# RWKV pairs: one of the two forms of a block inverse is updated, in half its columns, and the other is had by transposes

## The chip, the cores and the metric

One program runs on one core of a Trainium2 chip. The time is device microseconds (us) of that core, from the first to the last work of an execution; a kernel's time is the median of its runs. The engines work in parallel, each through its own list of instructions in order, and wait for one another by semaphores: PE (TensorE) multiplies matrices out of SBUF into PSUM, DVE (VectorE), ACT (ScalarE) and POOL (GpSimd) work on SBUF tiles (DVE and ACT also read PSUM), SP and POOL issue DMAs.

## What is computed

The program is two blocks, one after the other, on 256 tokens of 2048 channels. The first is two layers of linear attention, delta rule and differential attention, and the change leaves it alone. The second mixes with an RWKV scan, a convolution and a Fourier transform and ends with a feed-forward part. The change is in the RWKV scan: 16 heads of 64, over 256 context and then 256 own tokens, forward and backward.

```python
def wkv_scan(r, w, k, v, kk, a, s0, reverse):
    def step(s, inp):
        r_t, w_t, k_t, v_t, kk_t, a_t = inp
        sa = jnp.einsum('bhij,bhj->bhi', s, -kk_t)
        s = (s * w_t[:, :, None, :] + sa[..., None] * (kk_t * a_t)[:, :, None, :]
             + v_t[..., None] * k_t[:, :, None, :])
        return s, jnp.einsum('bhij,bhj->bhi', s, r_t)
    ...
def rwkv_mix(streams, s0, ln_w, ln_b, r_k, g_up):
    ...
    yf, sf = wkv_scan(r, wf, kf, v, kk, af, s0[0], False)
    yb, sb = wkv_scan(r, wb, kb, v, kk, ab, s0[1], True)
    y = yf + yb
    ...
def second_block(...):
    ...
    yc_rw, s_ctx = rwkv_mix(..., (s_zero, s_zero), *out_args)
    yx_rw, _ = rwkv_mix(..., s_ctx, *out_args)
```

## The kernel before

The scan is done in chunks of 64 tokens. Within a chunk the steps depend on one another through a unit triangular 64x64 matrix, and its inverse turns the recurrence into a few matrix products; from chunk to chunk only a 64x64 state is handed on. Two heads make a pair, one head on each half of the 128 partitions, and the 8 pairs are worked off one after the other. A pair has 8 cells (chunk and head) on each partition half and two directions d, so 32 systems of 64x64.

Of a direction's systems the tiles are: aT (the system), xm (its inverse), xmT (the inverse turned, that is transposed), mT (the part of aT that a level uses, by a mask), pm (a product copied out of PSUM), bT, rpk, kbv and wu (for what follows). Each is 128 partitions x 512 columns. PS is PSUM, eight banks of 512 columns.

The inverse is built by doubling. It starts with blocks of 2x2, and each of five levels joins two neighbouring blocks: with M the part that couples them, X becomes X - X M X. In the code a level has these steps, for d = 0 and d = 1 each:

- P: PE multiplies M and X (L1952, 64x64 products on quadrants of the array), into PSUM.
- ACT copies P to pm (`products`, L2255).
- X and Y: PE multiplies P from either side (L1969 for xm, L1971 for xmT), 64x64 columns each.
- DVE subtracts the two results from xm (L2631) and xmT (L2632), 512 columns each; level 5 needs xmT alone.
- POOL makes the next level's mT (`masks`, L1533) as soon as P has been read.

Ahead of level 1, PE makes scores of the pair (L1907 and L1909 for the system in both forms, L1919 and L1923 for the others) and, with the system copied, its turned form once more in another place (`turned_starts`, L1935); DVE masks them into the start values (`starts`). Level 5 also holds bT times the values (L1950), which ACT copies to kbv.

Around the levels, PE, DVE and ACT hold work of other pairs, written out by hand between the levels: head means and variances of the pair before (L1978 and the lines behind it) around levels 1 and 2, key sums of the next pair (L1866) after level 2, the decays of its two directions (L1858, L1859) after level 3 and inside or after level 4, key norms (L1873) after level 5. For each direction of decays ACT reads PE's result twice (a sigmoid and a multiple), DVE makes a running sum (`sums`, L2574 a scan, L2576 a product), and later ACT takes three exponentials; this goes into the scores of the next pair, which PE does after this pair's `solved` (L1991), eight dependent `steps` (L2001 to L2033), state updates (L2043) and outputs (L2053). The transposes by token (L1895) lie between the state updates.

Each engine works strictly in the order written; nothing reorders at run time apart from PE's weight loads. Semaphores named p_... count: p_P, p_Pc, p_Y, p_sub, p_xm, p_mask for the steps of a level, p_sig for the sigmoids, p_bvc for kbv. A matrix product in 32-bit floats is recorded as two MATMULs and two weight loads (LDWEIGHTS), a transpose as one of each.

## Time and profile before

| what | us |
|---|---|
| median of 3 runs | 3133.24 |
| lowest and highest run | 3127.13, 3143.53 |
| the profiled execution's own time | 3129.88 |
| its span in the trace | 3128.1 |

All rows are of that one profiled execution. Times in a timeline are microseconds from the start of the span, so that row times can be subtracted from one another. The RWKV pairs lie between about 1,635 and 2,165 us; the seven windows shown below each go from the scores of one pair to those of the next. The idle time before an instruction and what ended it stand in square brackets; "issue" there means that the engine waited for nothing that the profile shows. L numbers are lines of the kernel before.

### The profile page before, as it was taken

What the parts mean: (1) busy time and instruction counts of PE and PEld (TensorE: products, weight loads), DVE (VectorE), ACT (ScalarE), POOL (GpSimd) and SP (SyncE); (2) the same over time, 40 slices, a digit from 0 to 9 for tenths busy, and PEclk for the clock granted to TensorE, in tenths of its full rate; (3) what the DMA queues carried; (4) which work ended last, traced back from release to release, by engine and by line L of the source; (5) the groups of instructions that cost most, each with busy time, mean ns of one, the idle gap of its engine ahead of it and who ended that gap; (6) DMA issues with size and microseconds to landing.
All of it is one profiled execution on the core that took longest, in us unless ns stands there. A gap on an engine that the chain in (4) does not pass through costs nothing.

```text
span 3128.1 us, 68978 instructions
## 1 busy us (share of the span) xinstructions
PE 2990.7 (96%) x31912; PEld 2699.5 (86%) x31912; DVE 1603.6 (51%) x2262; ACT 566.0 (18%) x1041; POOL 1177.1 (38%) x657
## 2 busy tenths in 40 slices
PE   6999999999999999999998888888999999999998
PEld 5888888888888888787997777777999999999998
DVE  5755664656575324688914766765754131113232
ACT  1122111031110201100004555552110000000000
POOL 0000000100000000242772344443769787777775
PEclk9999999999999999999999999999999999999999
DMA  9954775955366445578640000002656444444442
GB/s 387 426 224 153 273 286 240 373 223 222 125 237 234 159 162 211 192 294 303 254 176 11 9 7 7 9 4 93 260 216 232 176 173 162 165 176 158 175 169 101
DMA packets 54160, 583.06 MB, mean 186 GB/s; under 512 B 6224, under 2 KB 6256, under 8 KB 8048
## 3 DMA queue, kind: packets, MB, share of 16 engines
q1 hardware_dynamic: 37856, 466.11, 39.3%
q0 software_dynamic: 16016, 112.54, 9.2%
q8 instruction: 251, 4.11, 0.5%
q14 instruction: 37, 0.30, 0.0%
HBM read 576.52 MB, written 2.10 MB: 185 GB/s over the span
## 4 chain that ended last, share of the span: by engine, by line
PE 90%; DVE 3%; issue 3%; DMA 2%; ACT 1%; POOL 0%; POOLq 0%; SPq 0%; DVEq 0%
PE PS L1766 28%; PE PS L371 20%; PE PS L1718 10%; PE PS L673 7%; PE PS L368 3%; PE PS L416 2%; PE PS L1952 2%; PE PS L1971 1%; PE PS L1969 1%; DMA ring<-in_w_start_dram 1%; PE PS L1895 1%; PE PS L1991 1%; PE PS L1783 1%; PE PS L1690 1%; PE PS L1701 1%
## 5 line engine op out<-in xcount | busy, mean ns | idle before, releaser
L371 PE MATMUL PS<-H,ring 128*128 128x256 f32 x2944 | 657.4, 381 | 0.0
L371 PEld LDWEIGHTS PS<-H,ring 128*128 128x128 f32 x2944 | 552.2, 190 | 82.7 <-issue 9.1
L1766 PE MATMUL PS<-H,ring 128*128 128x128 f32 x3424 | 402.8, 275 | 0.0
L1766 PEld LDWEIGHTS PS<-H,ring 128*128 128x128 f32 x3424 | 392.5, 192 | 0.1
L329 POOL DMA_DIRECT2D ring<-in_w_vec_dram x64 | 33.8, 528 | 860.2 <-DVE ring L930 659.1
L2463 DVE TENSOR_TENSOR W<-W,PS 128x256 f32<-128x256 f32 x58 | 24.4, 421 | 613.3 <-ACT W L2106 613.2
L1766 PE MATMUL PS<-H,W 128*128 128x128 f32 x2624 | 313.1, 275 | 0.0
L1766 PEld LDWEIGHTS PS<-H,W 128*128 128x128 f32 x2624 | 302.9, 192 | 0.0
L1585 POOL TENSOR_TENSOR W<-ring 128x1024 f32<-128x1024 f32 (+1 forms) x74 | 177.3, 2397 | 229.0 <-PE PS L1766 158.3
L673 PE MATMUL PS<-H,ring 128*128 128x256 f32 x1024 | 221.7, 379 | 2.9 <-DVE H L1228 2.9
L673 PEld LDWEIGHTS PS<-H,ring 128*128 128x128 f32 x1024 | 194.4, 190 | 30.0 <-issue 3.7
L1587 POOL TENSOR_TENSOR ring<-ring 128x1024 f32<-128x1024 f32 (+1 forms) x74 | 186.7, 2522 | 5.8
L1588 POOL TENSOR_TENSOR W<-W,ring 128x1024 f32<-128x1024 f32 (+1 forms) x74 | 180.7, 2442 | 0.0
L1590 POOL TENSOR_TENSOR W<-ring,W 128x1024 f32<-128x1024 f32 (+1 forms) x74 | 172.7, 2334 | 5.8
L1533 POOL TENSOR_TENSOR ring<-ring,W 128x512 f32<-128x512 f32 x64 | 89.0, 1408 | 185.0 <-PE PS L1952 185.0
L2199 ACT ACTIVATE ring<-PS 128x512 f32<-128x512 f32 (+2 forms) x248 | 130.6, 570 | 153.3 <-PE PS L1952 56.6
L2106 ACT ACTIVATE W<-PS 128x128 f32<-128x128 f32 (+2 forms) x60 | 17.0, 284 | 757.2 <-PE PS L1766 746.6
L930 DVE SCALAR_TENSOR_TENSOR ring<-ring,H 128x2048 f32<-128x2048 f32 x64 | 145.7, 2287 | 7.3 <-DMA ring<-in_w_vec_dram 6.6
L1718 PE MATMUL PS<-H,ring 128*128 128x128 f32 (+1 forms) x992 | 139.6, 302 | 5.5 <-DMA ring<-in_w_second_dram 5.4
L1718 PEld LDWEIGHTS PS<-H,ring 128*128 128x128 f32 x992 | 131.5, 195 | 12.2 <-DMA ring<-in_w_second_dram 5.5
L1766 PE MATMUL PS<-Pj,ring 128*128 128x128 f32 x1184 | 139.7, 275 | 0.0
L1766 PEld LDWEIGHTS PS<-Pj,ring 128*128 128x128 f32 x1184 | 135.9, 192 | 0.0
(472 smaller groups left out, 4915.6 us busy)
## 6 DMA issues: line engine op xcount, KB each, us to landing
ring<-in_w_second_dram SPq DMA_DIRECT2D x89, 2048.0 KB, 7.9
ring<-in_w_first_dram SPq DMA_DIRECT2D x68, 2048.0 KB, 7.9
ring<-in_w_vec_dram POOLq DMA_DIRECT2D x64, 1024.0 KB, 7.6
ring<-in_w_vec_dram SPq DMA_DIRECT2D x48, 1024.0 KB, 5.0
ring<-in_w_start_dram SPq DMA_DIRECT2D x16, 2048.0 KB, 15.8
Pj<-in_w_aside_dram SPq DMA_DIRECT2D x8, 2048.0 KB, 11.1
H<-in_w_vec_dram POOLq DMA_DIRECT2D x16, 1024.0 KB, 8.3
spare<-in_w_vec_dram POOLq DMA_DIRECT2D x16, 1024.0 KB, 8.6
```

What stands on the lines that cost most here:

```text
L368: mm = pe.matmul(PS[:, t % 2, half * TW:(half + 1) * TW], hT[:, k, half * P:(half + 1) * P], ring[:, t % 2, k, :], start=(k == 0), stop=(k ...
L371: mm = pe.matmul(PS[:, t % 2, half * T:(half + 1) * T], ring[:, t % 2, k, half * P:(half + 1) * P], hT[:, k, :], start=(k == 0), stop=(k = ...
L673: mm = pe.matmul(PS[:, 4 + 2 * (n % 2) + half, 0:T], ring[:, t % 2, k, half * P:(half + 1) * P], hT[:, k, :], start=(k == 0), stop=(k == K ...
L930: return v.scalar_tensor_tensor(out, a, s, b, op0, op1, **kw)
L1533: S("p_mask").inc(pool.tensor_tensor(mT[d], aT[d], each8(Ci(f"c_join{lev}")), ALU.mult))
L1585: sums.inc(pool.tensor_tensor(s_[:, 0], quarter(q, 2, nk), quarter(q, 3, nk), ALU.add))
L1587: sums.inc(pool.tensor_tensor(quarter(q, 2, nk), quarter(q, 0, nk), quarter(q, 2, nk), ALU.subtract))
L1588: sums.inc(pool.tensor_tensor(s_[:, 1], s_[:, 0], quarter(q, 0, nk), ALU.subtract))
L1590: sums.inc(pool.tensor_tensor(s_[:, 2], quarter(q, 1, nk), s_[:, 1], ALU.subtract))
L1718: mm = pe.matmul(in_regions(n % 2, wide, r), w[:, k * P:(k + 1) * P], at(m, k), start=(k == 0 and r // per not in opened), stop=(k == 7), ...
L1766: mm = pe.matmul(regions(bank2, r), w[:, k * P:(k + 1) * P], m[:, k, :], start=(first and k == 0 and r // 4 not in opened), stop=(last and ...
L2199: S(name).inc(act.activation(out_, in_, fn, **kw))
```

## The change

A level updates xmT alone. Its blocks of 2^lev columns come in two kinds, and the second of each two is all that a level alters; `joined` picks these, 256 of the 512 columns. Y multiplies 32 columns in place of 64 and X is gone. The product P is laid out so that all four quadrants of the array take part (`turned_at`, `by_parity`). xm is had by turning xmT: four transposes of 128x128 for each direction (`turned` in the program of PE), copied out of PSUM by DVE for d = 0 and by ACT for d = 1. There are five such turns for a pair, the first on the start values in place of `turned_starts`, and none after level 5.

With it go: only one start value for each direction on DVE; the first mT made by POOL, as a tenth mask; POOL's mask on rpk later, with a signal p_rpk of its own; the product of bT and the values in halves beside Y in levels 4 and 5, and its copies to kbv after p_sub of these levels; in ACT's `below` the copies of system and scores ahead of those to kbv. A direction's P now waits for one copy (p_xm or p_xs). Counting records of one pair, there are 280 MATMULs and 280 LDWEIGHTS fewer, out of 1,780 each.

The diff, without the tables of semaphores and their counts:

```diff
...
@@ -1406,6 +1406,9 @@
     GS = [flat(t)[:, 0:576].rearrange("p (m v) -> p m v", v=CH) for t in (Pj[:, 54:57, :], G[:, 5:8, :])]
     count = lambda lev, d: 2 * (lev - 1) + d + 1
     taken = lambda r, n: 2 * r + n + 1
+    turned_at = lambda u, c: 2 * (u // 2) + c
+    by_parity = lambda d: PS[:, 2 * d:2 * d + 2, 0:T]
+    joined = lambda t, lev: flat(t).rearrange("p (a s b) -> p a s b", s=2, b=1 << lev)[:, :, 1, :]
     seq = lambda t, d: t if d == 0 else t[:, :, ::-1]
 
 
@@ -1529,14 +1532,20 @@
 
         def masks(j, lev):
             for d in range(2):
-                need("p_P", j, count(lev - 1, d))
+                if lev == 1:
+                    need("p_aTc", j, d + 1)
+                else:
+                    need("p_P", j, count(lev - 1, d))
                 S("p_mask").inc(pool.tensor_tensor(mT[d], aT[d], each8(Ci(f"c_join{lev}")), ALU.mult))
 
-        def below(j, d):
+        def below_keys(j, d):
 
             need("p_BRr", j, d + 1)
             pool.tensor_tensor(bT[d], bT[d], each8(Ci("c_supper")), ALU.mult)
-            pool.tensor_tensor(rpk[d], rpk[d], each8(Ci("c_upper")), ALU.mult)
+
+        def below_reads(j, d):
+
+            return pool.tensor_tensor(rpk[d], rpk[d], each8(Ci("c_upper")), ALU.mult)
 
         def stream_back(j):
 
@@ -1559,12 +1568,15 @@
         ups(P, lambda ins: S("pair_loaded").inc(ins, 16))
         pool.wait_ge(S("cells_loaded").sem, 16)
         for j in range(NP2):
+            masks(j, 1)
             masks(j, 2)
-            below(j, 0)
+            below_keys(j, 0)
             masks(j, 3)
-            below(j, 1)
+            below_keys(j, 1)
             masks(j, 4)
+            below_reads(j, 0)
             masks(j, 5)
+            S("p_rpk").inc(below_reads(j, 1))
             if j < NP2 - 2:
                 need("p_z", j + 1, 2)
                 ups((j + 2) * P, lambda ins: ins.then_inc(S("pair_loaded").sem, 16))
...
@@ -1923,53 +1938,47 @@
                             mm = pe.matmul(PS[o_, 4 + 2 * d + par, T + n * CH:T + n * CH + CH], (pt, kt)[n // 2][r, t], RT(j, d)[r, tx], start=True, stop=True)
                 done(mm, "p_BR")
 
-        def turned_starts(j):
-
-            need("p_aTc", j, 2)
+        def turned(j, lev):
+
             for d in range(2):
-                kap, pt = flat(EV[d]), flat(AA[d])
-                for n in range(4):
-                    for c, o_ in enumerate(halves):
-                        t = slice(n * P + c * CH, n * P + c * CH + CH)
-                        for par, r in enumerate(halves):
-                            mm = pe.matmul(PS[o_, 2 + par, cell(4 * d + n)], pt[r, t], kap[r, t], start=True, stop=True)
-            done(mm, "p_xt")
+                if lev == 0:
+                    need("p_aTc", j, d + 1)
+                    need("p_x0", j, d + 1)
+                else:
+                    need("p_sub", j, count(lev, d))
+                for k in range(4):
+                    mm = pe.transpose(PS[:, 2 * d + k // 2, k % 2 * P:k % 2 * P + P], flat(xmT[d])[:, k * P:(k + 1) * P], ident)
+                done(mm, "p_xt")
 
         def level(j, lev, between=None):
-            if lev == 1:
-                turned_starts(j)
             for d in range(2):
-                if lev == 1:
-                    need("p_xs", j, d + 1)
-                else:
-                    need("p_mask", j, count(lev - 1, d))
-                    need("p_xm", j, count(lev - 1, d))
+                need(("p_xm", "p_xs")[d], j, lev)
+                need("p_mask", j, count(lev, d))
                 for u in range(8):
-                    if lev == 5:
-                        for h in halves:
-                            bv = pe.matmul(PS[h, 2 + d, cell(u)], bT[d][h, u, :], VTok[d][h, u % 4, halves[u // 4]], start=True, stop=True)
-                    for h, g in zip(halves, other):
-                        mm = pe.matmul(PS[h, d, cell(u)], mT[d][g, u, :], xm[d][g, u, :], start=True, stop=True)
-                if lev == 5:
-                    done(bv, "p_bv")
+                    g = halves[u % 2]
+                    for c, h in enumerate(halves):
+                        at = turned_at(u, c)
+                        mm = pe.matmul(PS[h, 2 * d + u % 2, cell(u // 2)], mT[d][g, at, :], xm[d][g, at, :], start=True, stop=True)
                 done(mm, "p_P")
             if lev == 1:
                 need("p_BRr", j, 1)
             for d in range(2):
                 need("p_Pc", j, count(lev, d))
-                if lev > 1:
-                    need("p_sub", j, count(lev - 1, d))
-                if lev == 1:
-                    need("p_x0", j, d + 1)
+                if lev == 5:
+                    need("p_bvc", j, d + 1)
                 if d and between:
                     between()
                 for u in range(8):
-                    if lev < 5:
-                        for h, g in zip(halves, other):
-                            pe.matmul(PS[g, 2 + d, cell(u)], xmT[d][h, u, :], pm[d][h, u, :], start=True, stop=True)
+                    if lev >= 4 and u < 4:
+                        w = 4 * (lev - 4) + u
+                        for h in halves:
+                            pe.matmul(PS[h, 4 + d, cell(4 + u)], bT[d][h, w, :], VTok[d][h, u, halves[lev - 4]], start=True, stop=True)
                     for h in halves:
-                        mm = pe.matmul(PS[h, 4 + d, cell(u)], pm[d][h, u, :], xmT[d][h, u, :], start=True, stop=True)
+                        out = PS[h, 4 + d, u * 32:(u + 1) * 32].rearrange("p (a b) -> p a b", b=1 << lev)
+                        mm = pe.matmul(out, pm[d][h, u, :], joined(xmT[d][h, u:u + 1, :], lev), start=True, stop=True)
                 done(mm, "p_Y")
+            if lev < 5:
+                turned(j, lev)
 
         def head_means(j):
             need("p_yread", j, 2)
@@ -1985,7 +1994,7 @@
         def solved(j):
             for d in range(2):
                 need("p_sub", j, count(5, d))
-                need("p_bvc", j, d + 1)
+                need("p_bvc", j, d + 3)
                 for u in range(8):
                     for h in halves:
                         mm = pe.matmul(PS[h, 4 * d + u // 4, (u % 4) * P:(u % 4 + 1) * P], xmT[d][h, u, :], kbv[d][h, u, :], start=True, stop=True)
@@ -2011,6 +2020,7 @@
                             mm = pe.matmul(PS[hs, sb_ + c, cell(n)], wu[d][rr, 4 * par + n, 0:64], PTok[d][rr, n, hs], start=True, stop=True)
                 done(mm, "p_rhs")
                 if d:
+                    need("p_rpk", j, 1)
                     need("p_rt", j, 1)
                 elif j < NP2 - 1:
                     need("p_kk", j + 1, 1)
@@ -2068,6 +2078,7 @@
         for r in range(4):
             by_token(0, r)
         scores(0)
+        turned(0, 0)
         for j in range(NP2):
             after, before = j < NP2 - 1, j > 0
             level(j, 1)
@@ -2094,6 +2105,7 @@
             outputs(j)
             if after:
                 scores(j + 1)
+                turned(j + 1, 0)
         head_means(NP2 - 1)
         head_vars(NP2 - 1)
 
@@ -2241,24 +2253,34 @@
                 need("p_tokT", j, taken(r, n))
                 f("p_tokc", t[d], PS[:, 2 + n, :].rearrange("p (a b) -> p a b", b=P), ACT.Copy)
 
+        def turned(j, lev):
+
+            need("p_xt", j, count(lev + 1, 1))
+            f("p_xs", flat(xm[1]).rearrange("p (b c) -> p b c", b=2), by_parity(1), ACT.Copy)
+
         def below(j):
 
+            for d in range(2):
+                need("p_aT", j, d + 1)
+                f("p_aTc", aT[d].rearrange("p (r n) b -> p r (n b)", r=2), PS[:, 2 * d:2 * d + 2, 0:T], ACT.Copy)
+            for d in range(2):
+                need("p_BR", j, d + 1)
+                f("p_BRr", br[d], PS[:, 4 + 2 * d:6 + 2 * d, :].rearrange("p r (w c) -> p r w c", w=2), ACT.Copy)
             need("p_tokc", j, 8)
             for d in range(2):
                 f("p_act", kbv[d].rearrange("p (r n) c -> p n r c", r=2)[:, :, :, 0:64], Ktok_[d].rearrange("p n (r c) -> p n r c", r=2), ACT.Copy)
-            for d in range(2):
-                need("p_aT", j, d + 1)
-                f("p_aTc", aT[d].rearrange("p (r n) b -> p r (n b)", r=2), PS[:, 2 * d:2 * d + 2, 0:T], ACT.Copy)
-                need("p_BR", j, d + 1)
-                f("p_BRr", br[d], PS[:, 4 + 2 * d:6 + 2 * d, :].rearrange("p r (w c) -> p r w c", w=2), ACT.Copy)
+            turned(j, 0)
 
         def products(j, lev):
             for d in range(2):
                 need("p_P", j, count(lev, d))
-                f("p_Pc", pm[d], PS[:, d, :].rearrange("p (a b) -> p a b", b=CH), ACT.Copy)
-                if lev == 5:
-                    need("p_bv", j, d + 1)
-                    f("p_bvc", kbv[d][:, :, 64:P], PS[:, 2 + d, :].rearrange("p (u c) -> p u c", c=64), ACT.Copy)
+                f("p_Pc", pm[d].rearrange("p (k b) c -> p b k c", b=2), by_parity(d).rearrange("p b (k c) -> p b k c", c=CH), ACT.Copy)
+            if lev < 5:
+                turned(j, lev)
+            if lev >= 4:
+                for d in range(2):
+                    need("p_sub", j, count(lev, d))
+                    f("p_bvc", kbv[d][:, 4 * (lev - 4):4 * (lev - 3), 64:P], PS[:, 4 + d, T:2 * T].rearrange("p (u c) -> p u c", c=64), ACT.Copy)
 
         def squares(j):
             need("p_yc", j, 1)
@@ -2608,30 +2630,30 @@
                 o.settle()
             o.do(v.tensor_tensor(EN[d], TMP[d], EN[d], ALU.mult), last)
 
+        def turned(o, j, lev):
+            need("p_xt", j, count(lev + 1, 0))
+            o.do(v.tensor_copy(flat(xm[0]).rearrange("p (b c) -> p b c", b=2), by_parity(0)), S("p_xm"))
+
         def starts(j):
             o = Order(v, own, j)
             for d in range(2):
                 need("p_AX", j, d + 1)
-                o.do(v.tensor_tensor(per_head(mT[d]), heads(2 * d, 0), each(Ci("c_join1")), ALU.mult))
-                o.do(v.tensor_tensor(per_head(xm[d]), heads(2 * d, T), each(Ci("c_join0t")), ALU.mult), S("p_aT"))
-                o.settle()
-                o.do(stt(xm[d], xm[d], -1.0, all8(Ci("c_ident")), ALU.mult, ALU.add), S("p_xs"))
-            need("p_xt", j, 1)
-            for e in range(2):
-                o.do(v.tensor_tensor(per_head(xmT[e]), heads(2, e * T), each(Ci("c_join0")), ALU.mult))
+                o.do(v.tensor_tensor(per_head(xmT[d]), heads(2 * d, T), each(Ci("c_join0")), ALU.mult), S("p_aT"))
             o.settle()
-            for e in range(2):
-                o.do(stt(xmT[e], xmT[e], -1.0, all8(Ci("c_ident")), ALU.mult, ALU.add), S("p_x0"))
+            for d in range(2):
+                o.do(stt(xmT[d], xmT[d], -1.0, all8(Ci("c_ident")), ALU.mult, ALU.add), S("p_x0"))
+            turned(o, j, 0)
 
         def level(j, lev, between=None):
             o = Order(v, own, j)
             for d in range(2):
                 need("p_Y", j, count(lev, d))
-                if lev < 5:
-                    o.do(v.tensor_tensor(xm[d], xm[d], bankv(2 + d), ALU.subtract), S("p_xm"))
-                o.do(v.tensor_tensor(xmT[d], xmT[d], bankv(4 + d), ALU.subtract), S("p_sub"))
+                o.do(v.tensor_tensor(joined(xmT[d], lev), joined(xmT[d], lev),
+                                     PS[:, 4 + d, 0:T].rearrange("p (a b) -> p a b", b=1 << lev), ALU.subtract), S("p_sub"))
                 if d == 0 and between:
                     between()
+            if lev < 5:
+                turned(o, j, lev)
 
         def centred(j):
             o = Order(v, own, j)
```

On PE, this is the place between levels 3 and 4 of a pair, with the decays of the next pair's first direction (L1858, L1859) between them; before, X (L1969) and Y (L1971) alternate in twos, 16 times in a level, of which the ends stand here:

```order
L1971 MATMUL PS<-ring 64x64 x2
L1969 MATMUL PS<-ring 64x64 x2
L1971 MATMUL PS<-ring 64x64 x2
L1858 MATMUL PS<-Pj,W 128x512
L1859 MATMUL PS<-Pj,W 128x512
L1952 MATMUL PS<-ring 64x64 x32
L1969 MATMUL PS<-ring 64x64 x2
L1971 MATMUL PS<-ring 64x64 x2
```

After, on the same engine and place, from Y of level 2 over the key sums (L1878) and the first direction's decays (L1870, L1871) to P of level 4:

```order
L1978 MATMUL PS<-ring 64x32 x32
L1950 MATMUL PS<-con,ring 128x128 x8
L1878 MATMUL PS<-con,W 128x2 x4
L1961 MATMUL PS<-ring 64x64 x32
L1978 MATMUL PS<-ring 64x32 x32
L1950 MATMUL PS<-con,ring 128x128 x8
L1870 MATMUL PS<-Pj,W 128x512
L1871 MATMUL PS<-Pj,W 128x512
L1961 MATMUL PS<-ring 64x64 x32
```

The turns (L1950) close a level, so that whatever was written behind a level now stands behind its transposes too, the decays of both directions included; before, they stood behind X and Y.

On ACT, the end of a pair before, from the copies of P in level 4 to the copies of `solved` (128x4x64 x8); the rows on W and H serve the next pair, 128x8x64 are the copies to kbv:

```order
L2199 ACTIVATE ring<-PS 128x512 x2
L2199 ACTIVATE W<-W,small,rope 128x512
L2199 ACTIVATE H<-H 128x512
L2199 ACTIVATE W<-PS,rope 128x512 x2
L2199 ACTIVATE ring<-PS 128x512
L2199 ACTIVATE ring<-PS 128x8x64
L2199 ACTIVATE ring<-PS 128x512
L2199 ACTIVATE H<-PS 128x8x64
L2199 ACTIVATE W<-W,small,rope 128x512
L2199 ACT_TABLE_LOAD
L2199 ACTIVATE W<-W 128x512 x3
L2199 ACTIVATE ring<-PS 128x4x64 x8
```

After, on ACT, the same place from the turn of level 4 on (128x512 out of PS), where 128x4x64 to ring and to H are the copies to kbv of levels 4 and 5:

```order
L2211 ACTIVATE ring<-PS 128x512
L2211 ACTIVATE ring<-PS 128x4x64
L2211 ACTIVATE H<-PS 128x4x64
L2211 ACTIVATE W<-W,small,rope 128x512
L2211 ACTIVATE H<-H 128x512
L2211 ACTIVATE W<-PS,rope 128x512 x2
L2211 ACTIVATE ring<-PS 128x2x4x64 x2
L2211 ACTIVATE ring<-PS 128x4x64
L2211 ACTIVATE H<-PS 128x4x64
L2211 ACTIVATE W<-W,small,rope 128x512
L2211 ACT_TABLE_LOAD
L2211 ACTIVATE W<-W 128x512 x3
```

The copies to kbv of level 5 stood between the two copies of P, ahead of Y; they now stand behind both and wait for DVE's subtraction of level 5, and the product on W, the table load and the exponentials stand behind them.

## Rows read from the trace of the kernel before

**Rows 1.** The page: totals, busy time of each engine, instruction queue, chain by engine.

```profile
span 3128.1 us, 68978 instructions
...
PE 2990.7 (96%) x31912; PEld 2699.5 (86%) x31912; DVE 1603.6 (51%) x2262; ACT 566.0 (18%) x1041; POOL 1177.1 (38%) x657
...
q8 instruction: 251, 4.11, 0.5%
...
PE 90%; DVE 3%; issue 3%; DMA 2%; ACT 1%; POOL 0%; POOLq 0%; SPq 0%; DVEq 0%
```

**Rows 2.** Windows of pairs: busy us by engine (instructions), granted clock, DMA share, GB/s.

```profile
1872.50:1932.30 59.80, 50.17 (x1782) 43.98 (x1779) 40.96 (x76) 32.02 (x56) 25.28 (x22) 1.00 0.03 7
1932.30:1993.20 60.90, 51.59 (x1784) 44.86 (x1781) 41.67 (x76) 31.93 (x56) 25.89 (x22) 0.97 0.03 7
...
sum 416.70, PE 352.50 PEld 307.64 DVE 283.62 ACT 225.06 POOL 178.25; mean PE 50.36 PEld 43.95 DVE 40.52 ACT 32.15 POOL 25.46
```

**Rows 3.** PE's waits from 1700 to 2160: total, times, longest.

```profile
PE PS L1971 <- issue: 17.1, 19, 1.8
...
PE PS L1969 <- issue: 6.5, 6, 1.6
...
PE PS L1907 <- issue: 0.6, 1, 0.6
```

**Rows 4.** PE's timeline of one pair: start, duration, line, shape, records.

```profile
1878.95 1.09 PE L1935 MATMUL PS<-W 64*64 64x64 f32 x60
...
1888.20 2.07 PE L1952 MATMUL PS<-ring 64*64 64x64 f32 x63
...
1892.87 1.05 PE L1866 MATMUL PS<-con,W 128*128 128x2 f32 x8
...
1899.03 1.13 PE L1858 MATMUL PS<-Pj,W 96*128 96x512 f32 x2
...
1904.88 1.12 PE L1858 MATMUL PS<-Pj,W 96*128 96x512 f32 x2
...
1911.87 1.16 PE L1873 MATMUL PS<-con,H 128*128 128x128 f32 x8
...
1924.74 1.09 PE L1895 MATMUL PS<-con,W 128*128 128x128 f32 x8
```

**Rows 5.** DVE's timeline of the same pair.

```profile
1888.90 0.42 DVE L2641 TENSOR_TENSOR Pj<-PS,Pj 128x256 f32<-128x256 f32 x1
...
1902.35 2.18 DVE L2574 TENSOR_TENSOR_SCAN W<-con,W 128x512 f32<-128x512 f32 x1 [0.17 <-ACT W L2199]
1904.57 1.58 DVE L2576 TENSOR_TENSOR W<-W 128x512 f32<-128x512 f32 x1
1906.07 0.68 DVE L2631 TENSOR_TENSOR ring<-ring,PS 128x512 f32<-128x512 f32 x1
...
1911.69 1.28 DVE L2632 TENSOR_TENSOR ring<-ring,PS 128x512 f32<-128x512 f32 x2
```

**Rows 6.** ACT's timeline of the same pair.

```profile
1883.45 0.62 ACT L2199 ACTIVATE Pj<-Pj 128x512 f32<-128x512 f32 x1
1883.97 0.71 ACT L2199 ACTIVATE Pj<-Pj,rope 128x512 f32<-128x512 f32 x1
1884.59 0.71 ACT L2199 ACTIVATE W<-Pj,rope 128x512 f32<-128x512 f32 x1
...
1889.40 0.60 ACT L2199 ACTIVATE ring<-PS 128x512 f32<-128x512 f32 x1
...
1910.30 0.81 ACT L2199 ACTIVATE W<-W,small,rope 128x512 f32<-128x512 f32 x1
1911.13 1.28 ACT L2199 ACT_TABLE_LOAD   x1
1912.43 1.67 ACT L2199 ACTIVATE W<-W 128x512 f32<-128x512 f32 x3
1914.97 1.21 ACT L2199 ACTIVATE ring<-PS 128x256 f32<-128x256 f32 x4 [0.87 <-PE PS L1991]
```

21 lines of the change are left out of this document (12 added, 9 removed).

## The prediction

> **What bounds the kernel now.** I read the page first. PE is busy 96% of the span and makes 90% of the chain that ended last [rows 1], so PE's list sets the time; the change touches only the eight RWKV pairs, so I went to the windows by pair [rows 2]. Seven whole pairs take 416.7 us, 59.5 each, and in these PE is busy 50.4, DVE 40.5, ACT 32.2, POOL 25.5. So a pair has 9.2 us in which PE stands still, and no engine but PE is near its limit on average. Then the waits of PE [rows 3]: the fifteen rows that end in "issue" (the first and the last stand there) sum to 53 us over 7.7 pairs, 6.9 a pair, and those on lines of the levels (L1971, L1969, L1952, L1935, L1950) to 31.4, 4.1 a pair. "Issue" means no partner; what fits them is PE's own instruction stream. The page has 251 transfers of instructions with 4.11 MB [rows 1], 16 KB each, and PE has 63,824 instructions, 254 to a transfer. The waits lie where PE runs through instructions fastest (X and Y). So in the levels PE is limited by its array and by how fast instructions arrive; DVE and ACT keep pace behind it.
>
> **PE's own work in a level.** Prices from [rows 4], by the distance of records (duration less the 0.22 us that the last one takes, by the count). With all four quadrants in turn, L1935 takes (1.09 - 0.22)/60 = 14.5 ns a record. With two quadrants, L1952 takes (2.07 - 0.22)/63 = 29.4 ns. Before, a level has 64 records of P at 29.4 (1.88 us) and 128 of X and Y at 14.5 (1.86): 3.74. After, P has four quadrants: 64 x 14.5 = 0.93. Y keeps two quadrants but has 32 moving columns instead of 64. No row has such a product. Bounds: the weights stay 64 columns, so nothing is saved (29.4 ns, 1.88 us), or half is (14.7 ns, 0.94 us). The nearest rows: L1866, with 2 moving columns, takes 1.05 us for eight records, L1873 with 128 columns 1.16. Sixty-four times the columns cost a tenth more: the weight load sets the pace of a short product. I take 1.88 and keep 0.94 as a rival. The eight transposes cost what eight of L1895 cost, 1.09 with the tail, 0.95 without. Sum after: 0.93 + 1.88 + 0.95 = 3.76. PE's work in a level stays the same, with 560 instructions a pair fewer.
>
> So the gain can only be the waits for instructions (4.1 us a pair in the levels, which I let vanish, since PE will now be waiting for data often enough for instructions to get ahead), and the cost is in the chain. A rule of the Trainium skill speaks against reading the waits so: "Runtime: NRT & Kernel Launch", section "Instruction fetch mechanics", has crossing a 16 KiB block "mostly hidden". The 17.1 us on L1971 alone [rows 3] disagree, unless those waits have another cause; that is the fourth rival.
>
> **The chain of a level.** Before, P of the next level waits for DVE's X, which is ready while Y is still in work; two directions hide one another. After, a direction's chain in a level is: P, copy to pm 0.60 [rows 6], Y, subtraction 0.42 (256 columns, the L2641 row [rows 5]), transposes, copy to xm 0.60 to 0.68, P. From P's start of d = 0 to that of the next level, with about 0.2 us of tail from PE to a reader: P 0.47, tail 0.2, two copies 1.2 (ACT does both directions in turn), Y of d = 1 0.94, tail 0.2, subtraction 0.42, four transposes 0.48, tail 0.2, copy 0.65: 4.8 to 5.1 us, with PE idle for 1.1 to 1.3. Before, from P of level 2 (1888.20) to the decays (1899.03), [rows 4], two levels and the key sums took 10.83, so 4.9 a level without the 1.05 of the key sums. Levels 1 to 3 are a draw. ACT is in order: the three keys (0.62 + 0.71 + 0.71, [rows 6]) stand between the copies of levels 1 and 2, and a table load behind level 3's; I put 1.1 to 1.6 us of extra waiting there, against the vanished 4.1 less what the longer chain takes. Bounds -0.4 and +0.5 a pair; I take -0.2. POOL's extra mask at the start and DVE's one start value fewer (before, `starts` had two a direction, 0.6 each) go the same way, into these bounds: POOL is busy 25 of 60 us [rows 2].
>
> **Level 4: the decays.** Here the order matters. Before, the second direction's decays L1858 lie between Y of d = 0 and d = 1 or right after, and wait for sigmoid reads only; the distance between the two L1858 is 1904.88 - 1899.03 = 5.85 us [rows 4], in every pair. DVE meanwhile does the running sum of the first direction, ending at 1904.57 + 1.58 = 1906.15, 7.12 after the first L1858 [rows 5]; level 4's subtractions stand behind it (1906.07). That cost nothing, since PE went on to the second decays. After, PE must first do level 4's transposes, which wait for the subtractions, which stand behind the sum: 7.12 + 0.42 + 0.42 + four transposes of d = 1 and their wait (0.6 to 0.9) = 8.6 to 8.9 before the second L1871 group starts. Against 5.85: +2.75 to +3.05. The work behind it follows: level 5's P waits for the copy of the turn, but that hides under the decays (1.9 us). I take +2.9.
>
> **Level 5 and behind.** PE loses the turn of level 5 and the X that was never there; the subtraction is 0.42 + 0.42 instead of 1.28 [rows 5], but stands as before behind the second sum (now later by the same 2.9). I take +0.2, for the product with bT that now lies in Y, bounds 0 and +0.4. Then ACT: before, the copies to kbv were done under PE's products, and W (0.81), table load (1.28), exponentials (1.67) followed, and the copies of `solved` came 0.87 us after ACT was free [rows 6]. They began at 1914.97, 2.0 after the end of the subtractions (1911.69 + 1.28 = 1912.97 [rows 5]). After, the last kbv copy (0.42) waits for the last subtraction, and W, table and exponentials follow: 0.42 + 0.81 + 1.28 + 1.67 = 4.2 after it. That is +2.2; the subtraction itself ends up to 0.5 earlier behind its Y and key norms cover part: +1.6, bounds +1.0 and +2.2. PE's steps wait for exactly these copies.
>
> **Sum.** -0.2 + 2.9 + 0.2 + 1.6 = +4.5 us a pair, bounds +3.3 and +6.1. Seven pairs have a next pair; the last has no decays, and no exponentials, and gains the vanished waits, about -2. Together 7 x 4.5 - 2 = +29.5, from +21 to +41. The profiled execution took 3129.88, the median is 3133.24, 3.4 above: 3159.4 to 3162.7, and I say 3160.
>
> **Transposes and the clock.** The granted clock was 1.00 in six of seven windows and 0.97 in one, which took 60.9 us [rows 2]; a pair already has 32 transposes (L1895) and 9 us of idling in it. The Trainium skill, "TensorE: Matmul & The Clock Gate", "Part 4: PE-mode transpose", says that transposes don't count as busy time for the clock. By that rule 40 more a pair could pull the clock from 2.4 to 1.2 GHz, which the windows so far don't bear out. One dip like that of the 0.97 window costs 0.03 x 60.9 = 1.8 us; in each of eight pairs it would be 14.5 us: 3174.
>
> **The rivals.**
> First, Y at half price: 32 columns take 14.7 ns. Each level is 0.94 shorter on PE and by some 0.9 in the chain; level 4's is hidden behind DVE's sum. Levels 1 to 3 and 5 give back 3.6, so +0.9 a pair, 7 x 0.9 - 2 = +4: 3134 to 3137, no change to be measured. This is the case that ends on the other side; it decides by one number, Y's cadence, and the break-even with my bound (+0.5%) is at some 21 ns. For it: products do get dearer with columns, two records of 512 (L1858, 1.13 us) costing what eight of 128 do (L1873, 1.16) [rows 4]; against it L1866.
> Second, the waits overlap: half of the two big terms is covered (ACT's work finds a gap, the second decays come earlier than the sum allows): +2.3 a pair, 7 x 2.3 - 2 = +14, 3144 to 3147, same.
> Third, Y at half price and the waits for instructions outside the levels (2.8 a pair) vanish too, since 560 instructions fewer run ahead: 0.9 - 2.8 = -1.9 a pair, -15: 3115, faster.
> Fourth, the waits for instructions stay (the skill's rule, another cause): +4.5 + 4.1 = 8.6 a pair, +58: 3188 to 3191.
> Fifth, the clock falls in the turns: 3174.
>
> **How the numbers follow.** Forecast (3151 to 3174) 0.50; Y at half price 0.17; waits overlap 0.13; faster 0.08; waits for instructions stay 0.06; clock 0.06. A measurement of this kernel tells about 0.5% (15.7 us) from no change, so faster means under 3117.6 and slower over 3148.9. Slower: 0.50 + 0.06 + 0.06 = 0.62; same 0.17 + 0.13 = 0.30; faster 0.08. The range from 3130 to 3176 takes in the forecast, its bounds, both cases of "same" and the clock, and leaves out the faster case and the case of 3190, with a little of the edges.
>
> **What would show it.** The distance of the two decay products from 5.85 to 8.6 or more (right), or still about 6 (the level 4 term is wrong). The copies of `solved` beginning 4 us after the last subtraction of level 5, with PE waiting for ACT at the first step. Y's records 29 ns apart, or 15 (first rival). "Issue" waits in levels near zero, or as before (fourth rival). The granted clock in the windows of pairs. I am wrong if the pair windows stay under 61.7 us (59.5 + 2.2), whatever the rest does.

## The result and the profile after

| | us |
|---|---|
| kernel before, median of 4 runs (3127.13 to 3143.53) | 3132.93 |
| kernel after, median of 4 runs (3165.00 to 3173.65) | 3167.78 |
| ratio, 95% interval | 1.0103 (1.0089 to 1.0117) |
| profiled execution of after, own time | 3173.65 |

Slower by 35 us, where 27 were forecast (3160 against the median of 3133). The page of after, which answers [rows 1]:

```profile
span 3171.9 us, 64489 instructions
...
PE 3030.5 (96%) x29672; PEld 2729.3 (86%) x29672; DVE 1541.3 (49%) x2190; ACT 583.2 (18%) x1097; POOL 1199.0 (38%) x673
...
q8 instruction: 233, 3.82, 0.5%
...
PE 81%; DVE 6%; ACT 4%; DMA 4%; issue 3%; POOL 1%; POOLq 0%; SPq 0%; DVEq 0%
```

PE has 2240 records fewer and is busy 40 us longer. The windows by pair, columns as in [rows 2] (the number behind the busy times is the granted clock):

```profile
1763.30:1828.50 65.20, 56.48 (x1506) 49.14 (x1503) 34.71 (x67) 34.09 (x63) 28.51 (x24) 0.90 0.03 6
1828.50:1895.60 67.10, 59.43 (x1503) 52.25 (x1500) 34.27 (x67) 34.32 (x63) 28.56 (x24) 0.85 0.02 6
1895.60:1956.00 60.40, 50.91 (x1500) 43.58 (x1497) 34.61 (x67) 33.85 (x63) 28.48 (x24) 1.00 0.02 6
...
sum 458.30, PE 389.94 PEld 336.62 DVE 233.25 ACT 238.62 POOL 197.48; mean PE 55.71 PEld 48.09 DVE 33.32 ACT 34.09 POOL 28.21
```

Seven pairs take 458.3 us, 65.5 each against 59.5 in [rows 2]: +5.9, where 4.5 were forecast. (This execution is the slowest of the four, 44 us over the profiled one of before, so its pairs show somewhat more than the 35 us of the medians.) But one pair ran at a granted clock of 1.00, and it took 60.4. The other six had 0.85 to 0.95 and took 64.1 to 68.8. So most of the loss is the clock. The first pair cut in three shows how:

```profile
1697.50:1715.50 18.00, 13.25 (x530) 11.96 (x528) 6.54 (x9) 9.86 (x17) 10.04 (x8) 1.00 0.01 4
1715.50:1729.10 13.60, 13.60 (x160) 11.44 (x156) 3.02 (x7) 4.49 (x7) 3.72 (x3) 0.50 0.01 1
1729.10:1763.30 34.20, 28.60 (x800) 24.50 (x801) 19.09 (x42) 19.92 (x40) 14.39 (x13) 1.00 0.04 9
```

For 13.6 us PE ran at 1.2 instead of 2.4 GHz. Ahead of that, it was busy 13.25 of 18.0 us, in scores and levels 1 and 2. The same products on PE's timeline, first in that stretch, then in the pair at full clock:

```profile
1720.80 3.62 PE L1978 MATMUL PS<-ring 64*64 64x32 f32 x64
1724.36 1.97 PE L1950 MATMUL PS<-con,ring 128*128 128x128 f32 x8
...
1914.38 0.95 PE L1878 MATMUL PS<-con,W 128*128 128x2 f32 x8
1915.27 1.16 PE L1961 MATMUL PS<-ring 64*64 64x64 f32 x64
1917.45 2.06 PE L1978 MATMUL PS<-ring 64*64 64x32 f32 x64 [1.02 <-ACT ring L2211]
1919.43 1.25 PE L1950 MATMUL PS<-con,ring 128*128 128x128 f32 x8
1920.52 1.02 PE L1870 MATMUL PS<-Pj,W 96*128 96x512 f32 x2
...
1924.53 0.33 PE L1975 MATMUL PS<-ring 64*64 64x64 f32 x4 [1.04 <-ACT ring L2211]
...
1925.40 0.72 PE L1978 MATMUL PS<-ring 64*64 64x32 f32 x20
...
1927.48 1.22 PE L1950 MATMUL PS<-con,ring 128*128 128x128 f32 x8
1928.54 1.02 PE L1870 MATMUL PS<-Pj,W 96*128 96x512 f32 x2
...
1935.71 1.16 PE L1885 MATMUL PS<-con,H 128*128 128x128 f32 x8
...
1941.50 0.34 PE L2010 MATMUL PS<-ring 64*64 64x64 f32 x8 [0.98 <-ACT ring L2211]
```

Sixty-four records of Y take 2.06 us at full clock, (2.06 - 0.22)/64 = 28.8 ns each, and 3.62 at half. Between the marks of that pair lie: from scores (1895.6) to key sums 18.8, to the first decays 6.1, to the second 8.0, to key norms 7.2, to the next scores (1956.0) 20.3. The six pairs of before at a clock of 1.00 take 59.3 us in the mean, (416.7 - 60.9)/6 by [rows 2], and have 20.3, 6.3, 5.85, 7.1, 19.8; the one of [rows 4], 59.8 long, has 20.4, 6.2, 5.85, 7.0, 20.4, and its last stretch is the longest of the six. So at full clock the change is worth -1.6 from the scores to the first decays (levels 1 to 3), +2.2 at level 4, nothing in level 5 and +0.5 behind the key norms: +1.1. That is one pair of after, but the pairs at full clock of e3_fill and e4_wide, below, have the same last three stretches (8.0, 7.2, 20.3).

PE's waits from 1700 to 2205 (total, times, longest), to be set against [rows 3]:

```profile
PE PS L1975 <- ACT ring L2211: 15.4, 16, 1.3
PE PS L1978 <- ACT ring L2211: 13.0, 12, 1.5
PE PS L1938 <- issue: 6.5, 5, 1.8
```

The waits for instructions in the levels are gone (none is left on L1950, L1961, L1975 or L1978). In their place PE waits for ACT's copy of P, ahead of Y, up to 1.5 us at a time. ACT's timeline of the pair at full clock says why:

```profile
1907.39 0.60 ACT L2211 ACTIVATE ring<-PS 128x512 f32<-128x512 f32 x1 [2.48 <-PE PS L1950]
1907.88 0.62 ACT L2211 ACTIVATE Pj<-Pj 128x512 f32<-128x512 f32 x1
1908.40 0.71 ACT L2211 ACTIVATE Pj<-Pj,rope 128x512 f32<-128x512 f32 x1
1909.01 0.71 ACT L2211 ACTIVATE W<-Pj,rope 128x512 f32<-128x512 f32 x1
1909.62 0.40 ACT L2211 ACTIVATE Pj<-Pj 128x256 f32<-128x256 f32 x1
1909.93 1.07 ACT L2211 ACTIVATE ring<-PS 128x512 f32<-128x512 f32 x2
...
1936.57 0.80 ACT L2211 ACTIVATE W<-W,small,rope 128x512 f32<-128x512 f32 x1
1937.39 1.28 ACT L2211 ACT_TABLE_LOAD   x1
1938.68 1.67 ACT L2211 ACTIVATE W<-W 128x512 f32<-128x512 f32 x3
1940.26 2.01 ACT L2211 ACTIVATE ring<-PS 128x256 f32<-128x256 f32 x7
```

The first row is the copy of level 1's turn. Keys and a square for other pairs follow it, and only then the two copies of P of level 2. Before the copy of the turn ACT had stood idle for 2.48 us. Ahead of level 3 it is a square root with its table load, ahead of levels 4 and 5 the sigmoids.

### The profile page after: what moved, and what is told of

It reads as the page before. It is cut to its first block, busy times and chain, and to the rows that moved or that the text cites. A ratio compares the mean times of both kernels' runs of the same rounds, so it can differ in the third digit from the quotient of the medians.

```text
span 3171.9 us, 64489 instructions
## 1 busy us (share of the span) xinstructions
PE 3030.5 (96%) x29672; PEld 2729.3 (86%) x29672; DVE 1541.3 (49%) x2190; ACT 583.2 (18%) x1097; POOL 1199.0 (38%) x673
## 4 chain that ended last, share of the span: by engine, by line
PE 81%; DVE 6%; ACT 4%; DMA 4%; issue 3%; POOL 1%; POOLq 0%; SPq 0%; DVEq 0%
PE PS L1778 28%; PE PS L371 20%; PE PS L673 7%; PE PS L1730 5%; PE PS L368 3%; PE PS L1978 2%; DMA ring<-in_w_vec_dram 2%; DVE ring L2381 2%; PE PS L416 2%; DMA ring<-in_w_start_dram 1%; ACT W L2211 1%; PE PS L1950 1%; ACT ring L2211 1%; PE PS L1907 1%; PE PS L1795 1%
## 5 line engine op out<-in xcount | busy, mean ns | idle before, releaser
L2211 ACT ACTIVATE ring<-PS 128x512 f32<-128x512 f32 (+2 forms) x296 | 151.8, 565 | 234.5 <-PE PS L1950 118.5
L1539 POOL TENSOR_TENSOR ring<-ring,W 128x512 f32<-128x512 f32 x80 | 109.3, 1384 | 188.3 <-PE PS L1961 113.0
L2381 DVE SCALAR_TENSOR_TENSOR ring<-ring,W 128x2048 f32<-128x2048 f32 x48 | 122.3, 2567 | 34.9 <-DMA ring<-in_w_vec_dram 34.7
```

The costliest lines, as they stand in the source:

```text
L1539: S("p_mask").inc(pool.tensor_tensor(mT[d], aT[d], each8(Ci(f"c_join{lev}")), ALU.mult))
L2211: S(name).inc(act.activation(out_, in_, fn, **kw))
L2381: v.scalar_tensor_tensor(w, w, 1.0, crow2[:, 0, :], ALU.mult, ALU.mult, accum_out=mod2[:, i - 64, 0:1]).then_inc(vec_done.sem, 1)
```

## Experiments

A first set asks what lowers the clock. IDLE: the waits. HALF: Y's 32 columns. TURNS: the transposes. Where the clock is the question, the window of a run's seven pairs stands with its result, from the first shown scores to the last. The time at the low level in a pair is 2 x (1 - clock) x length / 7; for after this is 2 x 0.09 x 458.3 / 7 = 11.8 us (the clock is rounded to 0.01, so this is good to 0.7). It is read from one execution of each kernel; over the whole program, every run of after has a clock of 0.980 to 0.984, those of e5_plain and w_dec 0.983 to 0.988, those of the other edits 0.986 to 0.995. Runs of different sets are compared by their ratios to the kernel before, which was run beside each (1% is 31 us).

```profile
1697.50:2155.80 458.30, 389.94 (x10453) 336.62 (x10453) 233.25 (x454) 238.62 (x441) 197.48 (x166) 0.91 0.02 6
```

**e3_fill.**

> The kernel after, with four more products of 128x128 (identity times identity, eight records, 0.95 us) into an unused part of PSUM, between P and Y of levels 1 to 4, where PE waits about 1.0 us for ACT's copies of P. Their result is read by nobody. In the trace of after the one pair with a granted clock of 1.00 takes 60.4 us and the mean of seven 65.5 with 0.91. Theory IDLE (PE's waits in the levels let the clock fall): clock back to 0.98 or more, pairs 60.4 to 61.5, total 3132 to 3145. Theory TURNS (the transposes let it fall) and theory HALF (the products of Y with 32 columns, which move half the data in the same time, let it fall): clock stays near 0.91, total 3165 to 3190.

```diff
+            if lev in (1, 2, 3, 4):
+                for _ in range(4):
+                    pe.matmul(PS[:, 4, T:T + P], ident, ident, start=True, stop=True)
             for d in range(2):
                 need("p_Pc", j, count(lev, d))
```

```profile
1699.40:2149.10 449.70, 392.29 (x10677) 338.29 (x10678) 223.40 (x454) 237.34 (x441) 198.47 (x166) 0.98 0.02 6
```

3164.51 us, ratio 1.0103 as after. The clock came back (2.6 us low a pair), the time did not: pairs at full clock took 63.2 instead of 60.4. In levels 3 and 4 the products fitted into the waits (6.1 and 8.0 between the marks, as in after), in levels 1 and 2 they did not (21.5 from scores to key sums instead of 18.8). Right on the clock for IDLE, wrong on the time. It doesn't exclude HALF, since it also adds columns.

**e4_wide.**

> The kernel after, with Y of levels 1 to 3 over all 64 columns again (the result is subtracted in the same half of the columns as before). If the weight load sets the pace, PE's time for Y stays (records 29 ns apart). Theory HALF: the clock comes back, pairs near 60.4 to 61, total 3132 to 3145. Theories IDLE and TURNS: no change, total 3160 to 3175. If instead columns set the pace (records of 32 columns at half price), this is slower by 0.9 us a level, 2.8 a pair, total 3190.

```diff
-                        mm = pe.matmul(out, pm[d][h, u, :], joined(xmT[d][h, u:u + 1, :], lev), start=True, stop=True)
+                        if lev < 4:
+                            mm = pe.matmul(PS[h, 4 + d, cell(u)], pm[d][h, u, :], xmT[d][h, u, :], start=True, stop=True)
+                        else:
+                            mm = pe.matmul(out, pm[d][h, u, :], joined(xmT[d][h, u:u + 1, :], lev), start=True, stop=True)
...
```

```profile
1697.00:2134.50 437.50, 363.55 (x10448) 311.12 (x10449) 230.84 (x454) 237.48 (x441) 197.44 (x166) 0.98 0.02 6
...
1907.88 2.08 PE L1979 MATMUL PS<-ring 64*64 64x64 f32 x64 [1.02 <-ACT ring L2214]
```

3147.46 us, ratio 1.0050 (1.0030 to 1.0069) where after has 1.0103: some 17 us less, from twice the columns; just above the range of HALF, well under that of IDLE and TURNS. Sixty-four records of 64 columns take 2.08 us, those of 32 took 2.06: the columns don't set the pace, as forecast. The waits are unchanged (1.02 before Y here too), yet the low time falls from 11.8 to 2.5 us a pair. So these waits alone don't lower the clock.

**e5_plain.**

> The kernel after, with each of the 40 transposes of a pair written as an ordinary product with the identity, two records instead of one: PE has 0.95 us more for each of the five turns, at most 4.75 a pair. Theory TURNS: the clock comes back, a pair goes from 65.5 to about 60.4 + 4 = 64.4, total 3155 to 3165. Theories IDLE and HALF: PE is busy in more of the level, so IDLE expects a little more clock; HALF expects none, and 4 us a pair more, total 3190 to 3200.

```diff
-                    mm = pe.transpose(PS[...], flat(xmT[d])[:, k * P:(k + 1) * P], ident)
+                    mm = pe.matmul(PS[...], flat(xmT[d])[:, k * P:(k + 1) * P], ident, start=True, stop=True)
```

```profile
1700.40:2177.80 477.40, 412.53 (x10729) 365.81 (x10730) 235.23 (x454) 238.79 (x441) 197.46 (x166) 0.94 0.02 6
```

3196.61 us, ratio 1.0194 (1.0166 to 1.0223), and the clock stays low (8.2 us a pair): HALF's total, with the little more clock that IDLE expected. Without a single transpose in the levels it still falls.

**b2_turns.**

> The kernel before, with eight dead transposes of the identity (0.95 us) behind Y of levels 1 to 4, into PSUM that nobody reads: no new wait, 32 transposes a pair more. Theory TURNS: the granted clock falls in the pairs as it does after, total 3170 to 3200. Theories IDLE and HALF: the clock stays at 0.98 or more; PE has 3.8 us a pair more, of which what falls into its waits costs nothing: total 3140 to 3163.

```diff
                 done(mm, "p_Y")
+            if lev < 5:
+                for n in range(8):
+                    pe.transpose(PS[:, n // 4, n % 4 * P:n % 4 * P + P], ident, ident)
```

```profile
1695.80:2114.80 419.00, 369.94 (x12632) 328.22 (x12633) 285.09 (x517) 224.41 (x394) 178.89 (x152) 1.00 0.02 7
```

3138.63 us, ratio 1.0022 (1.0010 to 1.0035) to before, a little under the range of IDLE and HALF, clock 1.00. As the cause by itself, TURNS has fallen from both sides. The Trainium skill ("TensorE: Matmul & The Clock Gate", "Part 4: PE-mode transpose") has transposes not count as busy time for the clock; 32 more of them a pair did not lower it here. The 3.8 us of them cost a pair 0.3 (419.0 against 416.7 for seven): PE's "issue" waits on the lines of the levels fell from 26.0 us in the seven pairs to 13.5.

A second set tests the chain, on e4_wide, where the clock disturbs little.

**w_dec.**

> The kernel of e4_wide (Y over 64 columns in levels 1 to 3, the clock mostly at 1.00; 3147 us, 61.1 us a pair at full clock), with the second direction's decays written between Y and the turns of level 4 instead of behind the turns. Theory SUM (the prediction's step: the turns of level 4 wait for DVE's running sum, and the decays stand behind them): the decays no longer wait, their distance falls from 8.0 to about 6, a pair loses 2 us, total 3133. Theory LIST (by the trace of after, the turns start 0.1 us after Y; the 8.0 us are PE's own list, decays 1.9, P 1.1, wait 1.0, Y with half of the bT product 3.0, turns 1.1): the distance falls by the 1.1 of the turns alone, and the wait for the copies behind the turns, which the decays covered, comes out: 0 to 0.9 us a pair slower, total 3147 to 3154.

```diff
-            if lev < 5:
+            if lev < 4:
                 turned(j, lev)
...
             if after:
                 decays(j + 1, 1)
+            turned(j, 4)
```

```profile
1699.00:2157.00 458.00, 378.37 (x10450) 328.29 (x10450) 232.53 (x454) 238.82 (x441) 197.22 (x166) 0.94 0.02 6
...
PE PS L1975 <- ACT ring L2215: 27.3, 16, 2.6
```

3174.86 us, ratio 1.0123, above both ranges. The two decays come 6.9 us apart at full clock, 8.0 less the turns' 1.1: LIST. SUM has fallen. The pair at full clock became 62.2, 1.1 longer (forecast 0 to 0.9): ACT's copies to kbv, products and sigmoids between the turn and the copies of P in level 5 had run while PE did the decays and now run while PE waits, and PE's waits on the first product of Y in levels 4 and 5 grew from 17.7 us in all (e4_wide) to 27.3. With it the clock fell too (0.94, 7.9 us a pair), which no theory had expected. All six low stretches of these pairs begin in level 5, during PE's wait of 2.6 us ahead of Y or within 2 us behind it; the four of 13.6 us in after begin in level 2, 1.4 to 2.0 us behind a wait of 1.3 to 1.5. The low stretch moved with the wait.

**w_bv.**

> The kernel of e4_wide with the second half of the bT product made between P and Y of level 5, into a bank of its own (behind ACT's sigmoids), and copied to kbv by ACT without the wait for DVE's last subtraction. Theory of the prediction (the copies to kbv, the product on W, the table load and the exponentials behind the subtraction delay the copies of solved by about 1.6): the time from key norms to the next scores goes from 20.3 to 19.3 or less, and the 0.94 us of the product fill a wait of PE: 1.5 to 2.5 us a pair less, total 3128 to 3137. Rival (the exponentials are bound by something else): under 0.5 us a pair, total 3144 to 3148.

```diff
+            if lev == 5:
+                if j < NP2 - 1:
+                    need("p_sig", j + 1, 4)
+                for d in range(2):
+                    for u in range(4):
+                        for h in halves:
+                            bv = pe.matmul(PS[h, 6, cell(4 * d + u)], bT[d][h, 4 + u, :], VTok[d][h, u, halves[1]], start=True, stop=True)
+                    done(bv, "p_bv")
...
```

3141.05 us, ratio 1.0013 (1.0002 to 1.0025), against 1.0050 of e4_wide. At full clock the time from key norms to the next scores went from 20.4 to 19.2, that from the second decays to key norms from 7.2 to 6.7, a pair from 61.1 to 59.7: 1.4, a little under what the prediction's theory gave, well over the rival's; the total lies between the two ranges. Key norms to the first step take 4.4 again.

**w_act.**

> The kernel of e4_wide with ACT's work for other pairs (keys, squares, the two square roots with their table load) in levels 1 to 3 written between the copies of P and the copy of the turn, instead of behind the latter. In the trace of after PE waits 1.0 to 1.3 us for ACT between P and Y in levels 2 and 3. Theory ORDER (ACT's other work in front of the copies of P makes these waits): each falls to 0.4, 1.2 to 1.6 us a pair less, total 3135 to 3140. Rival (the copy of the turn comes later instead, and P of the next level with it): total 3144 to 3150.

```diff
-            products(j, 1)
-            if after:
-                keys(j + 1)
-            ...
+            products(j, 1, [lambda: keys(j + 1)] if after else ())
+            products(j, 2, [lambda: squares(j - 1)] if before else ())
+            products(j, 3, ([lambda: head_roots(j - 1)] if before else []) + ([lambda: key_roots(j + 1)] if after else []))
...
```

(`products` calls these between its copies of P and the copy of the turn.) 3135.77 us, ratio 0.9997 (0.9984 to 1.0009), 0.5% under e4_wide; pairs at full clock went from 61.1 to 59.7, and PE's waits on Y of levels 1 to 3 from 1.5 us to 0.3 at most. ORDER.

**w_all.**

> The kernel of w_act with three more moves: ACT's first sigmoids between the copies of P and the turn of level 4; DVE's two running sums behind level 4's turn (the norm of the pair before ahead of it); and ACT's product on W and first exponential ahead of the copies to kbv of level 5. If the order on ACT and DVE is what is left of the loss: waits between P and Y of 0.4 in level 4, solved's copies 1.5 to 2 us earlier: another 2 to 3 us a pair, total 3115 to 3125, under the kernel before. If DVE's sums now come late for level 5: the gain there is lost, total 3130 to 3140.

```diff
+            products(j, 4, [lambda: sigmoids(j + 1, 0)] if after else ())
...
+            products(j, 5, [lambda: key_mixes(j + 1, 1), lambda: exponentials(j + 1, 0, (0,))] if after else ())
...
                 inverse(j - 1)
-            if after:
-                sums(j + 1, 0)
+                normed(j - 1)
             level(j, 4)
-            if before:
-                normed(j - 1)
             if after:
+                sums(j + 1, 0)
                 sums(j + 1, 1)
```

3122.10 us, ratio 0.9954 (0.9939 to 0.9970) to before. Pairs at full clock take 57.7, the decays lie 7.2 apart.

The last set goes back to the 32 columns of Y.

**n_all.**

> The kernel after with the order on ACT and DVE of w_all, and Y with 32 columns in all levels, as after has it. Tells how much of the clock's fall needs the half columns and how much the waits that the order makes. If HALF is enough alone: the clock stays near 0.91, pairs 57.7 + 5 = 63, total 3155 to 3165. If the clock falls only where long waits and half columns come together: slow stretches of 2 us a pair or less, as in w_all, total 3115 to 3130.


Its diff is that of w_act and w_all, on the kernel after.

```profile
1694.50:2098.00 403.50, 355.55 (x10449) 306.00 (x10450) 233.63 (x454) 240.65 (x441) 190.52 (x166) 1.00 0.02 6
```

3111.49 us, ratio 0.9935 (0.9920 to 0.9950) to before: 0.9935 against 1.0103, 53 us less than after by order alone, a little under its range, and with w_all_bv the fastest here. The clock stays at 1.00 with 32 columns in every level. HALF alone is not the cause either.

**n_act.**

> The kernel after with w_act's order alone: ACT's keys, squares and roots between the copies of P and the copy of the turn in levels 1 to 3. DVE's order, level 4, level 5 and the 32 columns of Y stay as after has them. Tells whether the waits of levels 2 and 3 (1.0 to 1.3 us between P and Y) are what the clock answers to. If so: slow stretches of 2 us a pair or less, pairs 59.7 at full clock as in w_act, total 3130 to 3140. If the clock needs level 4's and 5's waits gone too: slow stretches of 5 us a pair and more, total 3145 to 3160.


Its diff is that of w_act, on the kernel after.

```profile
1696.20:2114.60 418.40, 359.30 (x10448) 308.18 (x10449) 231.23 (x454) 238.92 (x441) 197.27 (x166) 0.99 0.02 6
...
PE PS L1975 <- ACT ring L2211: 16.1, 16, 1.3
PE PS L1978 <- ACT ring L2211: 4.0, 16, 0.3
```

3131.65 us, ratio 0.9993 (0.9980 to 1.0005) to before. The waits on Y's first levels fell to 0.3 at most, those of levels 4 and 5 stayed, and the clock was back. ACT's rows at level 2 read

```profile
1767.10 0.60 ACT L2211 ACTIVATE ring<-PS 128x512 f32<-128x512 f32 x1 [0.74 <-PE PS L1950]
1768.62 1.08 ACT L2211 ACTIVATE ring<-PS 128x512 f32<-128x512 f32 x2 [0.92 <-PE PS L1961]
```

The copies of P now wait for PE, where PE waited for them.

**b3_half.**

> The kernel before, with X and Y of each level over the 32 columns that the level alters (and DVE subtracting 256 columns instead of 512), no transposes, P and the order as before. Theory HALF: the records of X and Y stay 14.5 ns apart, and the granted clock falls in the levels as it does after, total 3145 to 3185. If the clock doesn't fall here: the products' time or DVE's shorter subtractions give something back, total 3120 to 3135, and half columns alone are not the cause.

```diff
+    flank = lambda t, lev, s: flat(t).rearrange("p (a s b) -> p a s b", s=2, b=1 << lev)[:, :, s, :]
-                            pe.matmul(PS[g, 2 + d, cell(u)], xmT[d][h, u, :], pm[d][h, u, :], start=True, stop=True)
+                            pe.matmul(flank(PS[g, 2 + d:3 + d, cell(u)], lev, 0), xmT[d][h, u, :], flank(pm[d][h, u:u + 1, :], lev, 0), start=True, stop=True)
...
```

```profile
1704.30:2121.60 417.30, 358.43 (x12409) 314.25 (x12410) 252.75 (x517) 223.71 (x393) 179.28 (x152) 0.97 0.02 7
...
1773.16 0.26 PE L1970 MATMUL PS<-ring 64*64 64x32 f32 x2
...
1773.75 0.25 PE L1970 MATMUL PS<-ring 64*64 64x32 f32 x2
```

From the first to the second of these rows of X lie 40 records of X and Y, 0.59/40 = 14.75 ns each: the pace stayed.

3133.99 us, ratio 1.0009 (0.9995 to 1.0022). The clock fell some (3.6 us low a pair, where before has 0.5), much less than after. Pairs at full clock took 58.5, 0.8 less than before's 59.3, which the clock took back. The total is in the second forecast's range; the clock lies between the two.

**w_all_bv.**

> w_all and w_bv together: the second half of the bT product between P and Y of level 5, where w_all still has 0.7 us of wait a level (11.0 us in 15 waits on the first product of Y in levels 4 and 5). Gain adds: 0.5 to 1 us a pair less than w_all's 3122, total 3114 to 3118. If it does not add (the exponentials were all that held solved back): 3120 to 3124.


Its diff is that of w_all and w_bv. 3113.42 us, ratio 0.9929 (0.9913 to 0.9946) against 0.9954 of w_all, 8 us less: the second gain adds, but less than alone (pairs at full clock from 57.7 to 57.2, where w_bv gave 1.4).

## Why the prediction was right, and where it was not

The time, 3160, and the direction were near; the sum behind them was not. Step by step:

- **PE's work in a level**: right. Y's records stand 28.8 ns apart and their columns don't set the pace (e4_wide, b3_half), and the first and third rivals fall with that. Busy time in a pair at full clock is 50.9 against 50.4.
- **The waits for instructions in the levels**: right, they vanished, and the fourth rival fell. That they are waits for instructions, which the prediction argued from counts, the trace of before bears out: all 62 "issue" waits of PE from 1700 to 2160 end 1.2 to 1.6 us after a 16 KB transfer of its instruction queue has ended, and 109 such transfers begin in that time. The Trainium skill's "mostly hidden" ("Runtime: NRT & Kernel Launch", "Instruction fetch mechanics") doesn't describe before, where 62 of 109 show as waits. After, the 31.4 us of them on lines of the levels went to none; elsewhere they stayed (21.8 us before and after).
- **Levels 1 to 3**: mis-sized. -0.2 was forecast, -1.6 measured at full clock, although PE waited 2.3 us for ACT there in that pair, more than the 1.1 to 1.6 allowed for. Which other part was priced too dear, the runs don't tell.
- **Level 4**: the size was near (+2.2 for +2.9), the cause was wrong. I let the turns wait for DVE's running sum. The rows of DVE show that the sum was over before Y was:

```profile
1925.52 1.57 DVE L2598 TENSOR_TENSOR W<-W 128x512 f32<-128x512 f32 x1
1927.02 0.97 DVE L2651 TENSOR_TENSOR ring<-ring,PS 128x256 f32<-128x256 f32 x2
...
1935.83 0.42 DVE L2651 TENSOR_TENSOR ring<-ring,PS 128x256 f32<-128x256 f32 x1 [0.98 <-PE PS L1978]
```

  The first subtraction did stand behind the sum, 0.9 us after its Y (1925.40 + 0.72), but PE was then still in Y of d = 1, and went from there to the turns (1927.48) without a gap. What makes 8.0 is PE's list, with the turns' 1.1, and the 1.04 us that Y waited for ACT; w_dec showed it.
- **Level 5 and behind**: the mechanism was right and its size near; a gain behind it was left out. The copies of `solved` began 4.0 us after the last subtraction (1940.26 against 1936.25; 4.2 forecast), PE waited 0.98 for them, and key norms to the first step grew from 4.4 to 5.8: +1.4 where +1.6 was forecast. But from the first step to the next scores the six pairs of before take 15.4 in the mean, this one 14.5, so that key norms to the next scores grew by 0.5. The gain doesn't come of the delay: in w_bv and n_all, where the first step is back at 4.4, the rest takes 14.7 in most pairs. Waits for instructions in the steps, 1.2 to 2.3 us a pair before and none in this pair, are part of it; the runs don't split it further. The +0.2 for level 5 itself came out as nothing.
- **The clock**: this was the fifth rival, at 0.06 and 1.8 us a pair. It was 5 us a pair: 65.5 on average, 60.4 at full clock. The size came from the one window at 0.97 of before; after has eight low stretches in seven pairs. The transposes, which the prediction named as the reason, are not it by themselves (b2_turns, e5_plain). The forecast's +4.5 was met by a full-clock chain of +1.1 and by the clock. That the sum came out is chance: by the sign that the prediction set itself, a pair under 61.7 us, the chain at full clock failed.

What lowers the clock is settled only in part. Both edits that keep the other thing as it is bring it back: wide products with the same waits (e4_wide, 2.5 us low a pair), short waits with the same narrow products (n_act 1.2, n_all 0.0). Narrow products without the waits, in the kernel before, lower it a little (b3_half, 3.6). So in the first three levels the two act together. In w_dec a longer wait brought the fall back (7.9) with wide products in levels 1 to 3, but ahead of a Y of level 5 that kept its 32 columns; no run has long waits and wide products in all levels. Which property of the work the chip answers to was not measured, and dead products (e3_fill) fit both.

## What to carry to other kernels

Where a step gets a new copy on an in-order engine, look at what stood behind the old one: work for others that used to fill an idle stretch now stands ahead of the next step's first copy. Moving those rows between the copies of P and the copy of the turn was worth 1.1% (n_act, 34 us, most of it by the clock: at full clock a pair went from 60.4 to 59.1) and turned a loss of 1.0% into none, with DVE's and the other ACT rows into a gain of 0.65% (n_all). And compare windows of the same granted clock before giving a cause: at full clock this change cost 1.1 us a pair, not 5.9.

## What was not expected of the hardware

- TensorE went to its lower level for stretches of up to 13.6 us in the middle of pairs (the rows from 1715.5), six pairs of seven, and a single pair of the same program not at all. All eight low stretches of the seven pairs began within 2.5 us behind a wait of PE of 1.0 to 1.8 us.
- In the kernel before, 62 of 109 transfers of PE's instructions showed as waits, 53 us in 460.
- Products with 32 instead of 64 columns cost the same time in two quadrants (28.8 ns) and in four (14.75 ns, b3_half; 14.5 in [rows 4] with 64), and went with more time at the low clock.
- A kernel with more columns to move was 0.5% faster than the one with fewer (e4_wide against after), but not where the waits were short (w_all 0.9954, n_all 0.9935).
